# Output projection of a hybrid layer: inverse root by logarithm and exponential, and the last tile's routing ahead of its cast and low part

## The reference

```python
mix = einsum('bnc,cd->bnd', mixed, p['w_out'])
x = x + g1 * mix
h = modulate(rmsnorm(x, norm2_g), sh2, sc2)      # h * (1 + scale) + shift
def rmsnorm(x, g):
    y = xf * lax.rsqrt(jnp.mean(xf * xf, axis=-1, keepdims=True) + EPS)
    ...
def expert_choice_ffn(h, p):
    logits = einsum('bnd,de->bne', h, p['router'])
    probs = softmax(logits, axis=-1)
    gate, idx = lax.top_k(probs.transpose(0, 2, 1), cap)   # 256 rows for each of 16 experts
    ...
```

## Time and profile before

| what | value |
|---|---|
| median of 3 runs | 2297.72 us (2297.08 to 2298.5) |
| the profiled execution | 2297.26 us, its span 2295.4 us |
| busy: PE, DVE, ACT, POOL | 2170.8, 1590.8, 1038.6, 499.6 us |
| mean granted clock of TensorE | 0.976 |
| output projection stage | about 976 to 1177 us of the span |

### The profile page before, as it was taken

How to read it: one execution, slowest core, us unless ns; L and a number is a source line. 1 busy time by engine, 2 the same in 40 slices (tenths; PEclk the granted TensorE clock), 3 DMA queues, 4 the chain that set the end, 5 groups by cost and what they waited for, 6 DMA issues and landing times. The chain is left out here.

```text
span 2295.4 us, 38798 instructions
## 1 busy us (share of the span) xinstructions
PE 2170.8 (95%) x14917; PEld 1453.6 (63%) x14917; DVE 1590.8 (69%) x2230; ACT 1038.6 (45%) x1333; POOL 499.6 (22%) x538
## 2 busy tenths in 40 slices
PE   7799999999999999899966999999999999999995
PEld 3444444444878787645525777777777777777772
DVE  2749999784679687765565666766666666766666
ACT  3611011455666666545542444454444444553444
POOL 1710001012657566300021111101111011101111
PEclk9899999999999999899978999999999999999998
DMA  9431002454020221375545677666676677667676
GB/s 348 99 73 35 17 23 88 140 170 127 6 56 13 82 57 24 117 266 173 170 166 193 209 242 228 232 225 220 221 239 223 214 232 237 227 222 232 222 238 266
DMA packets 216932, 377.16 MB, mean 164 GB/s; under 512 B 38147, under 2 KB 79619, under 8 KB 216333
## 3 DMA queue, kind: packets, MB, share of 16 engines
q1 hardware_dynamic: 198702, 317.38, 40.8%
q0 software_dynamic: 16528, 56.47, 9.1%
q10 hardware_dynamic: 1616, 2.16, 0.3%
HBM read 313.44 MB, written 62.54 MB: 164 GB/s over the span
## 5 line engine op out<-in xcount | busy, mean ns | idle before, releaser
L90 PE MATMUL pgu<-xlo,mwhi 128*128 128x256 bf16 x2048 | 558.3, 273 | 0.0
L89 PE MATMUL pgu<-xhi,mwhi 128*128 128x256 bf16 x2048 | 558.3, 273 | 0.0
L91 PE MATMUL pgu<-xhi,mwlo 128*128 128x256 bf16 x2048 | 558.3, 273 | 0.0
L2470 DVE TENSOR_TENSOR mwlo<-mwst,mwhi 128x2048 bf16<-128x2048 f32 x187 | 427.0, 2283 | 0.0
L2367 ACT ACTIVATE mwhi<-mwst 128x2048 bf16<-128x2048 f32 x186 | 350.8, 1902 | 0.0
L2375 ACT ACTIVATE thb<-pgu 128x256 f32<-128x256 f32 x128 | 49.0, 383 | 547.4 <-PE pgu L91 547.3
L690 DVE SCALAR_TENSOR_TENSOR co<-u,taps,co 128x1984 f32<-128x1984 f32 (+22 forms) x120 | 234.1, 1951 | 3.7
L2481 DVE SCALAR_TENSOR_TENSOR thb<-thb,pgu 128x256 f32<-128x256 f32 x128 | 53.8, 420 | 258.2 <-ACT thb L2375 258.2
L2303 POOL TENSOR_TENSOR mpflag<-mpflag 1x1 f32<-1x1 f32 x46 | 37.5, 815 | 846.2 <-DVE ysb L2497 579.3
L89 PEld LDWEIGHTS pgu<-xhi,mwhi 128*128 128x128 bf16 x2048 | 200.4, 98 | 24.5
L90 PEld LDWEIGHTS pgu<-xlo,mwhi 128*128 128x128 bf16 x2048 | 200.4, 98 | 24.5
(11 more groups left out here) (400 smaller groups left out, 4326.9 us busy)
## 6 DMA issues: line engine op xcount, KB each, us to landing
mwst<-in_w_gate SPq DMA_DIRECT2D x32, 2048.0 KB, 8.9
mwst<-in_w_up SPq DMA_DIRECT2D x32, 2048.0 KB, 7.9
mwst<-in_w_down SPq DMA_DIRECT2D x32, 2048.0 KB, 7.9
wst<-in_w_in SPq DMA_DIRECT2D x28, 512.0 KB, 5.9
big<-in_ada_w SPq DMA_DIRECT2D x5, 2048.0 KB, 13.9
s_rows<-row SPq DMA_DIRECT2D x16, 520.0 KB, 5.8
u<-in_ada_w SPq DMA_DIRECT2D x8, 1024.0 KB, 6.1
xt<-in_x SPq DMA_DIRECT2D x16, 512.0 KB, 4.4
```

Source lines behind the costliest of these rows:

```text
L89: nc.tensor.matmul(out, lh, rh, start=(first and k == 0), stop=False)
L90: nc.tensor.matmul(out, lh, rl, start=False, stop=False)
L91: ins = nc.tensor.matmul(out, ll, rh, start=False, stop=(last and k == n - 1))
L2470: nc.vector.tensor_tensor(wlo[:, b, ks], wst[:, b % NS, ks], whi[:, b, ks], ALU.subtract)\
```

## The change

The root is taken by two activations on ACT, a logarithm and an exponential of minus one half of it, in place of a square root on ACT and a reciprocal on DVE. At the end of the stage, the routing of tile 15 stands ahead of that tile's cast on ACT and ahead of its low part on DVE; for this DVE's `route` is cut in two, and the second write of the probabilities is now `share`, which for tile 15 comes after `low`.

```diff
 # ACT, front
-  activation(st[:, p, 1:2], st[:, p, 0:1], ACT.Sqrt, bias=K["eps"][:, 0:1], scale=1.0 / D).then_inc(sd_ok[p], 1)
+  activation(st[:, p, 1:2], st[:, p, 0:1], ACT.Ln, bias=K["eps"][:, 0:1], scale=1.0 / D).then_inc(sd_ok[p], 1)
+  wait(act, sd_ok[p], n + 1)
+  wait(act, hn_ok[p], n)
+  activation(st[:, p, 2:3], st[:, p, 1:2], ACT.Exp, scale=-0.5).then_inc(rs_ok[p], 1)
 # ACT, last
   partial(1, n)
+  route(1, n)
   cast(1, n)
-  route(1, n)
 # DVE, front
-  wait(dve, sd_ok[p], n + 1)
-  reciprocal(st[:, p, 2:3], st[:, p, 1:2]).then_inc(rs_ok[p], 1)
   wait(dve, rs_ok[p], n + 1)
 # DVE, route is cut
+  def share(p, n):
       tensor_scalar(prob[:, p, :], pe_[:, p], nm[:, p, 2:3], None, ALU.mult).then_inc(pr_ok[p], 1)
 # DVE, last
   route(NT - 3, 1, n - 1)
+  share(1, n - 1)
   route(NT - 2, 0, n)
+  share(0, n)
+  route(NT - 1, 1, n)
   low(1, n)
-  route(NT - 1, 1, n)
+  share(1, n)
```

More of the change, by code:

```diff
@@ L1810, in front @@
                     wait(act, ss_ok[p], n + 1)
-                    nc.scalar.activation(st[:, p, 1:2], st[:, p, 0:1], ACT.Sqrt, bias=K["eps"][:, 0:1], scale=1.0 / D)\
+                    nc.scalar.activation(st[:, p, 1:2], st[:, p, 0:1], ACT.Ln, bias=K["eps"][:, 0:1], scale=1.0 / D)\
                         .then_inc(sd_ok[p], 1)
+                    wait(act, sd_ok[p], n + 1)
+                    wait(act, hn_ok[p], n)
+                    nc.scalar.activation(st[:, p, 2:3], st[:, p, 1:2], ACT.Exp, scale=-0.5).then_inc(rs_ok[p], 1)
                 def cast(p, n):
@@ L1886, in front @@
                 def front(t, p, n):
-                    wait(dve, sd_ok[p], n + 1)
-                    nc.vector.reciprocal(st[:, p, 2:3], st[:, p, 1:2]).then_inc(rs_ok[p], 1)
                     wait(dve, rs_ok[p], n + 1)
@@ L1918, in step @@
                         route(t - 2, p, n - 1)
+                        share(p, n - 1)
                     if have[1]:
```

## The result

| kernel | median (runs) | kernel before, same chip | ratio [95%] |
|---|---|---|---|
| the change | 2306.05 us (6; 2304.86 to 2309.61) | 2297.34 us (6) | 1.0046 [1.0035, 1.0056] |

A forecast was written before the change was run, and what follows sets the result against it. PE was taken to bound the stage's middle, stalling once the h2T copy exceeds its margin. Start 3.15, steps 3 to 15 6.23 and end 1.0 sum to 10.4 us: 2308.1 us from the 2297.72 median, range 2304.5 to 2311.5.

The forecast's parts named there:

- the signs that I had named: Forecast wrong if logits show no wait, a load shows a gap beside it, or step 4's cast still waits for the store.
- Table loads: On ACT: 32 loads of 1283 ns, two in each tile's front, none before the router's exponential, where 14 and 14 stood.
- The rival of no loads: Not slower: no loads in the fronts, middle unchanged, copy pr 1.6 us earlier at the end; 2296.1 us, 3 in 100.
- Price per tile: ACT in the middle: 1.70 us from logarithm to the h2T copy, 1.50 more than before, taking 0.20 for the exponential.
- the rival at 2327: A drain at each table load adds 19 us more; 1 in 100.
- PE's margin: PE's logits start 1.15 us after the h2T copy ends, 0.95 in some steps; each stall is 1.55 less that.
- The rival in which PE doesn't stall in the middle: Each step has 0.5 us more margin than read, so only start and end cost: 4.2 us, 2301.9; 6 in 100.
- Steps 3 to 15: PE's stalls waiting for h2T in these steps, mostly 0.40 or 0.60 us each, sum to 6.23 us.
- DVE's side: The reciprocal goes and h2 starts later, 1155.69 in place of 1154.38, but ends before it is needed: nobody waits.
- Step 2, the start: New loads in the first fronts make tile 1's h2T copy 4.02 us late; PE stalls 3.15 us.
- the clock as a rival: PE's clock falls because of the gaps, 0.4 us in 12 us; 2 in 100.
- The end: After tile 15's projection: late h2 and row 13's store lose 2.6 us, reordering saves 1.6; net 1.0 us later.

The follow-up runs named there:

- e3: The change with one hand-written load, at the stage's start, of a table holding both logarithm and exponential: 2293.29 us, 0.9994 of before; stage 187.30 us.
- e11: The change with one table of both functions loaded at the stage's start, repeated on another chip: 2294.39 us, 0.9995 of before; stage 187.86 us.
- e6: The kernel before with two 128x1024 copies added on ACT between root and h2T, not in tile 15: 2312.81 us, ratio 1.0074.
- e5: The kernel before with one 128x1024 copy added on ACT between root and h2T, not in tile 15: 2298.40 us, ratio 1.0012.
- e2: The kernel before with only the root changed to logarithm and exponential, the end in the old order: 2310.22 us, ratio 1.0059.
- e7: The change run again, unaltered, for another profile: 2309.09 us, 1.0068 of before; stage 203.10 us.
- e10: The change run a third time, unaltered: 2310.23 us, 1.0062 of before; stage 203.10 us.
- e4: The change, but tiles 0 and 1 keep square root and reciprocal: 2304.94 us, 1.0041 of before; stage 198.65 us.
- e8: The change with one table of both functions loaded at the stage's start, and the old order of the end: 2295.34 us, 0.9999 of before.
- e1: The kernel before with only the end reordered, square root and reciprocal kept: 2295.49 us, 1.0000 of before; stage 189.02 us.

## Why the prediction held, and where it did not

The change is slower, by the mechanism forecast, and 2306.05 lies in the range. That the point forecast of 2308.1 was so near is in part luck: the sum of 10.4 was 2.4 us too small for the stage, and the stages ahead happened to be 5.2 us quicker in the profile of the change. Of the signs that I had named, none spoke against it: every logit waits, no load has a gap beside it, and step 4's cast no longer waits for the store.

- *Table loads.* Right: 16 at L1811, 16 at L1815, none at L1833. The rival of no loads asked what their absence would give; e3 and e11 gave 3.0 and 2.5 us of stage where it said 1.6.
- *Price per tile.* Right: 1.52 against 1.50, with 0.20 for the exponential. No run shows the drain of the rival at 2327, nor the 19 us that it was to add: in the timeline of step 14 the loads take 1.28 us each with 0.01 to 0.02 us ahead and behind, and the whole stage lost 12.75 us.
- *PE's margin.* Right within about 0.1 us: 0.93 in step 2 gave a gap of 3.27 for a forecast 3.15, and in step 14 the change and e6 both leave 1.09 or 1.10 unpaid, where I had read 1.15 and 0.05. (The copy of tile 1 comes 4.11 us late, not 4.02: step 1 is 1.32 longer in place of 1.24, and from the squares to the copy it is 2.79.) The rival in which PE doesn't stall in the middle fell; the kernel that does what it describes is e5, at a delay 0.57 us shorter.
- *Steps 3 to 15.* 6.23 forecast, 6.25 measured, but two errors cancel. Steps 4 to 14 cost 0.6 less than I had them: 0.3 in steps 4 and 5, where before itself had 24.36 us in one profile and 24.14 in the other, and 0.3 in the loop, for which I have no cause. Step 15 cost 0.92 for 0.40, by a chain that I missed under "DVE's side", where I wrote that h2 is later and "Nobody waits". In the timeline of the end the cast of tile 14 waits 0.66 us for h2 (L1896), the low part of tile 14 for that cast, and gated(15) stands behind the low part on DVE. In the loop the row maximum and exponential lie between and hide this; the end has no routing ahead of the cast.
- *Step 2, the start.* The step that failed. The gap was right, but I counted only the gap. In e2, which has the gap and keeps the full clock, steps 1 and 2 take 20.72 us, 3.33 more than before; the change takes 22.40. The 1.68 us between them are the projection matmuls at half rate, every 0.43 us in place of 0.21 or 0.22. I had put this term at nothing. I had priced the clock as a rival for gaps of 0.4 us in the middle, where the granted clock did stay at 1.00, and had not asked it of my own 3.15 us gap.
- *The end.* 1.49 for 1.0. The late h2 and routing came as forecast, but the last turn took 1.97 us at a granted clock of 0.50 behind a gap of 3.77 us, as against 1.09 before:

```profile
1166.47 1.09 PE L1961 MATMUL ptp<-ident,h 128*128 128x128 f32 x8 [1.22 <-DVE h L1895]
```

  So tile 15's routing was last, not row 13's store. By estimate, without these 0.88 us the cast would stand at 1179.9 and, with the 4.05 us that the store took before, be held to 1180.2, which is the forecast's end. It is the same step that failed: a long gap priced without the clock behind it.

## What to carry to other kernels

The loads of the kernel before cost steps 6 to 14 nothing, for ACT had slack *at that place in its order* (108.45 us with them and, in e3, without). On the way to the bound engine each load of the change added its full 1.28 us, and what exceeded that engine's margin (1.10 us in step 14) was paid. So count the loads in the compiled order, and read the bound engine's margin for what stands behind them. A change of function that looks like a saving (one reciprocal less) has to be priced by its table; where one table serves both functions, as in e3, see that the compiled program uses it: this took 15.8 us off the stage. And price a long gap on TensorE with the case that what follows runs at a lower clock; behind a gap of 3.3 to 3.5 us it was 0.51 to 0.54 in three profiles of four here.

## What the runs showed of the hardware

- In step 2, after gaps on PE of 3.27, 3.50 and 3.36 us, three profiles (after, e7, e10) show a granted clock of 0.51 to 0.54 in a stretch of 3.4 or 3.5 us behind them, and e2 shows 1.00 behind a gap of 3.40. What decides between them I can't say: in the microseconds ahead of the stage the clock differed from run to run (from 960 to 964 us 0.50 in the profile before, 0.57 in e10 and 1.00 in the profile after), the one rule that I tried on it failed in e10, and no experiment varied it. At the end of the stage all five profiles with the gap of 3.77 us (after, e2, e4, e7, e10) show 1.97 us for the turn behind it, and before, which has no such gap, 1.09. That the gap itself brings the fall is likely by this, and by the other nine profiles, which have no such gap in step 2 and kept 1.00 there (e6 with one of 1.14 us), but it isn't shown.
- The instruction that loads a table took 1283 ns wherever these profiles were read, and a 128x1 exponential without an operand for its bias 203 ns against 294 ns for the 128x1 logarithm with one.
- Where the last cast waited for it, the store of row 13 took between 2.8 (e8) and 4.7 us (e1) from its issue to that cast, at the same place in the program. That spread of 1.9 us is more than the reordering gained (1.31 and 0.91).
